# Expert gate/up of a mixture-of-experts layer: high and low token halves stacked in one stationary operand, two weight passes, the halves folded by a product

## The reference

```python
def expert_block(args):
    xb, e = args
    hb = jax.nn.silu(xb @ w_gate[e]) * (xb @ w_up[e])
    return hb @ w_down[e]
```

## Time and profile before

| | |
|---|---|
| runs shown, median of 3 | 2478.95 us (2477.13 to 2481.66) |
| the profiled execution: span from first to last instruction | 2474.9 us |
| the part before the first expert product | 1206 us |
| PE busy | 2220.9 us, 90% of the span |
| DVE busy | 1447.8 us, 58% |
| ACT busy | 1201.1 us, 49% |
| loads by SyncE's queue | 530.43 MB |

### The profile page before, as it was taken

One profiled execution on the slowest core, in us unless ns is written; L12 is line 12 of the kernel. 1 busy time (PEld: TensorE's weight loads), 2 busy tenths in 40 slices (PEclk: granted clock), 3 DMA queues, 4 the chain that ended last, 5 costly groups with the idle time before them and its releaser, 6 DMA issues.

```text
span 2474.9 us, 36169 instructions
## 1 busy us (share of the span) xinstructions
PE 2220.9 (90%) x13825; PEld 2005.5 (81%) x13825; DVE 1447.8 (58%) x1219; ACT 1201.1 (49%) x1121; POOL 233.6 (9%) x237
## 2 busy tenths in 40 slices
PE   2999999999999999995599999999999999999970
PEld 2989999999999999985477787787777778778750
DVE  8443232222222243337587887887887887887858
ACT  3333232222122232224377777777777777777743
POOL 4000440000000010003101000000000000000004
PEclk9999999999999999996799999999999999999985
DMA  6334233333323244336399999999999999999944
GB/s 225 85 98 112 69 94 88 91 89 89 92 86 93 85 151 131 106 100 241 113 344 359 357 352 355 361 351 349 359 354 354 358 358 347 368 360 350 371 176 170
DMA packets 338329, 556.23 MB, mean 225 GB/s; under 512 B 13592, under 2 KB 179552, under 8 KB 315360
## 3 DMA queue, kind: packets, MB, share of 16 engines
q1 hardware_dynamic: 330848, 530.43, 61.5%
q0 software_dynamic: 7440, 25.25, 3.4%
HBM read 542.78 MB, written 29.62 MB: 231 GB/s over the span
## 4 chain that ended last, share of the span: by engine, by line
PE 83%; DVE 8%; ACT 4%; issue 3%; DMA 1%; DVEq 0%; SPq 0%; ACTq 0%; POOLq 0%; POOL 0%
PE ps L1558 79%; ACT ehi L796 2%; PE ps L1787 2%; DVE hrow L1486 1%; DVE wlo L1109 1%; DVE eraw L1520 1%; PE ps L1750 1%; DMA rows<-in_x 1%; DVE rows L1130 1%; DVE nmr L1125 1%; PE ps L1795 1%; DVE xT_lo L1109 0%; ACT whi L796 0%; DVE eraw L1532 0%; DVE stats L1112 0%
## 5 line engine op out<-in xcount | busy, mean ns | idle before, releaser
L1109 DVE TENSOR_TENSOR elo<-eraw,ehi 128x2048 fp32r<-128x2048 f32 x380 | 856.6, 2289 | 146.6 <-ACT ehi L796 142.0
L796 ACT ACTIVATE ehi<-eraw 128x2048 fp32r<-128x2048 f32 x384 | 724.9, 1914 | 150.2 <-PE ps L1558 145.3
L1109 DVE TENSOR_TENSOR wlo<-raw,whi 128x1024 fp32r<-128x1024 f32 (+3 forms) x200 | 225.2, 1126 | 567.7 <-ACT whi L796 565.9
L796 ACT ACTIVATE whi<-raw 128x1024 fp32r<-128x1024 f32 (+3 forms) x200 | 191.6, 959 | 736.6 <-PE ps L1558 736.6
L1558 PE MATMUL ps<-act_hi,whi 128*128 128x264 f32 x2048 | 423.7, 287 | 18.7 <-DVE wlo L1109 13.4
L1558 PE MATMUL ps<-act_lo,whi 128*128 128x264 f32 x2048 | 422.0, 286 | 0.0
L1558 PE MATMUL ps<-act_hi,wlo 128*128 128x264 f32 x2048 | 421.8, 286 | 0.0
L1558 PE MATMUL ps<-ehi,xT_hi 128*128 128x512 f32 x1024 | 403.4, 394 | 4.7 <-DVE elo L1109 4.7
L1558 PE MATMUL ps<-ehi,xT_lo 128*128 128x512 f32 x1024 | 400.4, 391 | 0.0
L1558 PE MATMUL ps<-elo,xT_hi 128*128 128x512 f32 x1024 | 399.6, 390 | 0.0
L1558 PEld LDWEIGHTS ps<-act_hi,whi 128*128 128x128 f32 x2048 | 321.5, 189 | 21.2 <-DVE wlo L1109 12.1
(11 more groups left out here) (192 smaller groups left out, 2107.1 us busy)
## 6 DMA issues: line engine op xcount, KB each, us to landing
eraw<-in_w_gate SPq DMA_DIRECT2D x128, 1024.0 KB, 7.6
eraw<-in_w_up SPq DMA_DIRECT2D x128, 1024.0 KB, 7.8
eraw<-in_w_down SPq DMA_DIRECT2D x128, 1024.0 KB, 9.1
raw<-in_w_in SPq DMA_DIRECT2D x96, 512.0 KB, 3.8
raw<-in_w_out SPq DMA_DIRECT2D x32, 512.0 KB, 3.9
h_rows<-rows SPq DMA_DIRECT2D x8, 1024.0 KB, 7.3
raw<-in_w_branch_pool SPq DMA_DIRECT2D x16, 512.0 KB, 3.9
raw<-in_w_branch_fourier SPq DMA_DIRECT2D x16, 512.0 KB, 3.9
```

The costliest lines, as they stand in the source:

```text
L796: act.activation(dst, src, ACT.Copy, **kw).then_inc(done, 1)
L1109: dve.tensor_tensor(dst, src, hi, ALU.subtract).then_inc(done, 1)
```

## The change

- **Stacking.** xT becomes one buffer [128, 16, 2, 64]: for each of the 16 row pieces the 64 hi columns and the 64 lo columns of the tokens side by side, 128 stationary columns in all. Each weight half is then streamed once: ehi and elo, 2 matmuls where there were 3 (64 per round instead of 96). Bank rows 0 to 63 hold hi x w, rows 64 to 127 lo x w. lo x elo, which the kernel before leaves out, is now in the sum.
- **Fold.** ACT copies banks 0 and 1 to `gu` in SBUF. In the next round 8 small float32 products of gu with `fold` [128 x 64] (two identities on top of one another) add the halves and transpose in one step; the result, 4 x 64 columns of gate and as many of up, goes to bank 1. ACT makes `silT` = silu of the gate part, DVE `hraw` = silT * up part, ACT and DVE split hraw to hT_hi and hT_lo. silu and product so stand after the transposing step, on 256 columns instead of 512.
- **Loads.** gate_up gives partition p the rows 4p to 4p+3 of a chunk, one run of 8 KB. The tokens' columns must then be taken with a step of four: xT is made by 16 float32 products of `xrow[:, start:start+509:4]` with 64 columns of the identity, all before the down chunks, 8 pieces to a bank.
- **Order.** On ACT y_evac moves from behind ehi 3 to behind ehi 1; silu stands behind ehi 5, ht_split behind ehi 6; on DVE the gated product behind elo 5, the split behind elo 6. PE's first up product (chunk 4) waits for h_done (hraw written) instead of ht_lo.

The diff, cut to its core:

```diff
-    hrow = sb("hrow", [P, F], F32, 65536)
...
-    xT_hi = sb("xT_hi", [P, KC, P], F32R, 167936)
-    xT_lo = sb("xT_lo", [P, KC, P], F32R, 176128)
+    xT = sb("xT", [P, KC, 2, CAP], F32R, 167936)
+    gu = sb("gu", [P, 2, F], F32, 176128)
+    silT = sb("silT", [P, 4, CAP], F32, 180224)
+    hraw = sb("hraw", [P, 4, CAP], F32, 181248)
+    fold = sb("fold", [P, CAP], F32, 65536)
...
-    srow = sb("srow", [P, F], F32, 209088)
...
-            return w[0, bass.ds(e, 1), 512 * (i % 4):512 * (i % 4 + 1), :].rearrange("a (k p) n -> p (a k) n", p=P)
+            return w[0, bass.ds(e, 1), 512 * (i % 4):512 * (i % 4 + 1), :].rearrange("a (p k) n -> p (a k) n", p=P)
...
-                pool.wait_ge(xt_ready, 4 * b + 4)
+                pool.wait_ge(xt_ready, 2 * b + 2)
...
             def xt_evac(b, q):
-                act.wait_ge(xt_ready, 4 * b + q + 1)
-                copy(xT_hi[:, 4 * q:4 * q + 4, 0:CAP], used_cols(ps[:, 6 + q % 2, :]), xt_hi)
-            def ht_evac(b):
+                act.wait_ge(xt_ready, 2 * b + q + 1)
+                copy(xT[:, 8 * q:8 * q + 8, 0, :], xt_bank(q), xt_hi)
+            def gu_copy(b, a):
+                act.wait_ge(eused, number(b, 4 * a + 3) + (1 + ERING))
+                past(act, ht_ready, b)
+                copy(gu[:, a, :], ps[:, a, :], gu_done)
+            def silu(b):
                 act.wait_ge(ht_ready, b + 1)
-                copy(hT_hi[:, :, 0:CAP], used_cols(ps[:, 1, :]), ht_hi)
+                past(act, h_done, b)
+                act.activation(silT[:, :, :].rearrange("p c n -> p (c n)"), ps[:, 1, 0:4 * CAP], ACT.Silu).then_inc(silu_done, 1)
+            def ht_split(b):
+                act.wait_ge(h_done, b + 1)
+                copy(hT_hi[:, :, 0:CAP], hraw[:, :, :], ht_hi)
...
             def moe_round(b):
-                if not (isinstance(b, int) and b < 1):
-                    for i in range(4):
-                        ehi_chunk(b, i)
+                follows = not (isinstance(b, int) and b < 1)
+                if follows:
+                    ehi_chunk(b, 0)
+                    ehi_chunk(b, 1)
                 if not (isinstance(b, int) and b < 2):
                     y_evac(b - 2, number(b - 1, ECH - 1))
-                if not (isinstance(b, int) and b < 1):
-                    ht_evac(b - 1)
-                for i in range(4, 8):
-                    ehi_chunk(b, i)
-                act.wait_ge(eused, number(b, 3) + (1 + ERING))
-                past(act, h_done, b)
-                act.activation(srow[:, :], ps[:, 0, :], ACT.Silu).then_inc(silu_done, 1)
-                if not (isinstance(b, int) and b < 1):
+                if follows:
+                    ehi_chunk(b, 2)
+                    ehi_chunk(b, 3)
+                ehi_chunk(b, 4)
+                ehi_chunk(b, 5)
+                if follows:
+                    silu(b - 1)
+                ehi_chunk(b, 6)
+                if follows:
+                    ht_split(b - 1)
+                ehi_chunk(b, 7)
+                gu_copy(b, 0)
+                if follows:
                     for i in range(8, 12):
                         ehi_chunk(b, i)
-                for q in range(4):
+                gu_copy(b, 1)
+                for q in range(2):
                     xt_evac(b + 1, q)
...
             end = n_over + NE
             ehi_chunk(end, 0)
             ehi_chunk(end, 1)
-            ht_evac(end - 1)
+            silu(end - 1)
+            ht_split(end - 1)
             y_evac(end - 2, number(end, -1))
...
             def xt_evac(b, q):
-                dve.wait_ge(xt_hi, 4 * b + q + 1)
-                lo_of(xT_lo[:, 4 * q:4 * q + 4, 0:CAP], used_cols(ps[:, 6 + q % 2, :]),
-                      xT_hi[:, 4 * q:4 * q + 4, 0:CAP], xt_lo)
-            def ht_evac(b):
+                dve.wait_ge(xt_hi, 2 * b + q + 1)
+                lo_of(xT[:, 8 * q:8 * q + 8, 1, :], xt_bank(q), xT[:, 8 * q:8 * q + 8, 0, :], xt_lo)
+            def gated(b):
+                dve.wait_ge(silu_done, b + 1)
+                past(dve, ht_lo, b)
+                dve.tensor_tensor(hraw[:, :, :].rearrange("p c n -> p (c n)"), silT[:, :, :].rearrange("p c n -> p (c n)"),
+                                  ps[:, 1, 4 * CAP:8 * CAP], ALU.mult).then_inc(h_done, 1)
+            def ht_split(b):
                 dve.wait_ge(ht_hi, b + 1)
-                lo_of(hT_lo[:, :, 0:CAP], used_cols(ps[:, 1, :]), hT_hi[:, :, 0:CAP], ht_lo)
+                lo_of(hT_lo[:, :, 0:CAP], hraw[:, :, :], hT_hi[:, :, 0:CAP], ht_lo)
...
             def moe_round(b):
-                if not (isinstance(b, int) and b < 1):
+                follows = not (isinstance(b, int) and b < 1)
+                if follows:
                     for i in range(4):
                         elo_chunk(b, i)
-                if not (isinstance(b, int) and b < 1):
-                    ht_evac(b - 1)
-                for i in range(4, 8):
-                    elo_chunk(b, i)
-                if not (isinstance(b, int) and b < 1):
+                elo_chunk(b, 4)
+                elo_chunk(b, 5)
+                if follows:
+                    gated(b - 1)
+                elo_chunk(b, 6)
+                if follows:
+                    ht_split(b - 1)
+                elo_chunk(b, 7)
+                if follows:
                     for i in range(8, 12):
                         elo_chunk(b, i)
-                dve.wait_ge(silu_done, b + 1)
-                dve.wait_ge(eused, number(b, 7) + (1 + ERING))
-                past(dve, ht_lo, b)
-                dve.tensor_tensor(hrow[:, :], srow[:, :], ps[:, 1, :], ALU.mult).then_inc(h_done, 1)
-                for q in range(4):
+                for q in range(2):
                     xt_evac(b + 1, q)
-                if not (isinstance(b, int) and b < 1):
+                if follows:
                     gate_weights(b - 1)
-            for q in range(4):
+            dve.tensor_tensor(fold[:, :], ident[:, 0:CAP], ident[:, CAP:P], ALU.add).then_inc(fold_ready, 1)
+            for q in range(2):
                 xt_evac(0, q)
...
-            ht_evac(end - 1)
+            gated(end - 1)
+            ht_split(end - 1)
...
-            def xt(b, q):
-                if q == 0:
-                    pe.wait_ge(gathered, 16 * b + 16)
-                past(pe, xt_lo, 4 * b + q - 1 if q else 4 * b)
+            def xt(b):
+                pe.wait_ge(gathered, 16 * b + 16)
                 pe.wait_ge(pad_cols, 1)
-                for c in range(4):
-                    k = 4 * q + c
-                    last = pe.transpose(ps[:, 6 + q % 2, P * c:P * (c + 1)], xrow[:, P * k:P * (k + 1)], ident)
-                last.then_inc(xt_ready, 1)
+                for q in range(2):
+                    past(pe, xt_lo, 2 * b)
+                    for c in range(8):
+                        start = 512 * (2 * q + c // 4) + c % 4
+                        last = pe.matmul(xt_bank(q)[:, c, :], xrow[:, start:start + 509:4], ident[:, 0:CAP], start=True, stop=True)
+                    last.then_inc(xt_ready, 1)
             def ht(b):
-                pe.wait_ge(h_done, b + 1)
-                pe.wait_ge(pad_cols, 5)
-                for c in range(4):
-                    last = pe.transpose(ps[:, 1, P * c:P * (c + 1)], hrow[:, P * c:P * (c + 1)], ident)
+                pe.wait_ge(gu_done, 2 * b + 2)
+                pe.wait_ge(fold_ready, 1)
+                for a in range(2):
+                    for c in range(4):
+                        at_c = 4 * CAP * a + CAP * c
+                        last = pe.matmul(ps[:, 1, at_c:at_c + CAP], gu[:, a, P * c:P * (c + 1)], fold[:, :],
+                                         start=True, stop=True)
                 last.then_inc(ht_ready, 1)
             def down_product(b, i, k):
@@ -1809,34 +1825,30 @@
             def moe_round(b):
                 follows = not (isinstance(b, int) and b < 1)
                 for i in range(8):
-                    if i < 4:
-                        pe.wait_ge(xt_lo, 4 * b + i + 1)
+                    if i in (0, 2):
+                        pe.wait_ge(xt_lo, 2 * b + i // 2 + 1)
                     if i == 0:
-                        past(pe, silu_done, b)
+                        past(pe, gu_done, 2 * b)
                     if i == 2 and follows:
                         ht(b - 1)
                     if i == 4:
-                        past(pe, ht_lo, b)
+                        past(pe, h_done, b)
                     pe.wait_ge(elo_done, number(b, i) + 1)
                     for kk in range(4):
                         k = 4 * (i % 4) + kk
-                        last = product([ps[:, i // 4, :]], xT_hi[:, k, :], xT_lo[:, k, :],
-                                       [ehi[:, i % ERING, F * kk:F * (kk + 1)]],
-                                       [elo[:, i % ERING, F * kk:F * (kk + 1)]], k == 0, k == KC - 1)
+                        both = xT[:, k, :, :].rearrange("p a n -> p (a n)")
```

(28 more changed lines are left out.)

4 lines of the change are left out of this document (3 added, 1 removed).

## The result

| | before | change |
|---|---|---|
| median of 4 runs | 2478.04 us (2474.78 to 2481.66) | 2601.37 us (2598.68 to 2604.86) |
| span of the profiled execution | 2474.9 us | 2601.9 us |
| one expert round, mean of the 31 distances between gated products | 36.87 us | 40.63 us |
| one expert round, rounds 2 to 30, from first gate product to first gate product | 36.88 us | 40.97 us |

The ratio is 1.049 (95% interval 1.0463 to 1.0517). The change is slower by 5%, where I forecast 3% faster.

What follows compares the result with a forecast made beforehand. PE was taken to set the pace; rounds going from 36.87 to 33.30 us gave 107 less, start 5.6 less, end 2.3 more, clock 30 more: -80, 2394.6 us, given as 2398 after the runs' median, range 2360 to 2460.

Steps and rivals of the forecast that it cites:

- The loop: Expert round, last down product through yrow, ehi 2, elo 2 to 5, hraw, chunks 4 to 7, xT, down: 33.30 us.
- The loads are hidden: Expert-stage loads at 424 GB/s with gather and scatter: 31.5 us a round, under the 33.3 of the loop.
- the price of the xT products: Sixteen strided float32 products on PE per round, taken at 0.19 us each, 3.04 us in the loop.
- The prediction's own sign of being wrong: The prediction called itself wrong if, among other signs, PE's xT stretch took over 5 us.
- The break-even: Price of one strided xT product from which the change turns slower: 0.42 us.
- rival 5: The strided xT read costs four times, 0.76 us a product, 9.1 more per round: 2642 us; chance 0.08.
- rival 4: The strided xT read doubles the record, 3.0 us more per round: 2459 us; chance 0.13.
- clock term: PE's clock falls after the new stall in half of the rounds at 2 us, 1 us a round: 30 us more.
- If 367 stayed, 36.1: Expert-stage loads staying at 367 GB/s despite 8 KB runs, rounds of 36.1 us: 2453 us; chance 0.05.
- Start and end: Outside rounds 2 to 31: the start 5.6 us less, the end 2.3 us more.
- part of the rounds: PE's clock falls after the stall in only some rounds, the forecast case: 2398 us; chance 0.45.

Runs made afterwards that it cites:

- e1_contig: The change with contiguous xrow pieces and 2 KB runs again, stacking, fold and order kept: 2401.3 us, ratio 0.967.
- e3_transpose: The change with 14 of the 16 xT products made as one-pass transposes, 8 KB runs and step four kept: 2412.8 us, ratio 0.971.
- e6_fill: The change with 12 extra 512-column products on PE ahead of the wait for hraw: 2570.7 us, ratio 1.034.
- e7_both: e3_transpose with the order edit of e4_order added: 2323.3 us, ratio 0.937.
- e8_contig_order: e1_contig with the order edit of e4_order added: 2371.8 us, ratio 0.958.
- e4_order: The change with y_evac one chunk later and silu, product and split one chunk earlier on ACT and DVE: 2507.2 us, ratio 1.010.
- e10_double: e1_contig with every xT product made twice, the repeat writing the same values: 2528.5 us, ratio 1.020.
- e11_mix: e4_order with the sixteen strided xT products put one by one between the first down products: 2400.7 us, ratio 0.968.
- e2_step2: The change with 4 KB runs, so that xrow is read with a step of two elements: 2429.2 us, ratio 0.979.

## Why the prediction was wrong

**What held.** The gate and up products went from 96 to 64. The fold's eight products were put at 1.5 us and take 1.70. The loop is there as described: the trace shows yrow, ehi 2 right behind it, elo 2 to 5, hraw, then chunk 4. ACT and DVE around it, of one round:

```profile
1809.02 2.75 ACT L1044 ACTIVATE yrow<-ps,gcol 64x512 f32<-64x512 f32 x4 [1.51 <-PE ps L1571]
1811.66 7.32 ACT L783 ACTIVATE ehi<-eraw 128x2048 fp32r<-128x2048 f32 x4
```

```profile
1813.60 8.90 DVE L1114 TENSOR_TENSOR elo<-eraw,ehi 128x2048 fp32r<-128x2048 f32 x4 [3.77 <-ACT ehi L783]
1822.41 0.41 DVE L1471 TENSOR_TENSOR hraw<-silT,ps 128x256 f32<-128x256 f32 x1
```

DVE idle 3.77 us ahead of elo 2 (3.5 forecast), elo 2 to 5 in 8.90 (8.98), PE's stall 2.70 (about 3.0). From the last down product to chunk 4 the loop was put at 2.72 + 8.98 + 0.40 = 12.10 us; the gate products with the stall and the fold, which fill that time on PE, take 10.38 + 1.70 = 12.08. The loads are hidden, as said.

**The step that failed** is the price of the xT products: "I take 0.19, since the rows near it are the same operation". They were the same operation on a contiguous operand; the price under the step is 0.453, 7.26 us for the term put at 3.04. The prediction's own sign of being wrong, an xT stretch over 5 us, came. The break-even, which rival 5 gave as 0.42 us a product, was thus crossed, and the size lay between rival 4 (0.38) and rival 5 (0.76). That 0.42 left out the prediction's own clock term; with 1 us a round for it the break-even is (36.87 - 34.30 + 0.11) / 16 + 0.19 = 0.36. The argument against rival 5, that the weight load is partly hidden, was true but proved little: of 329 ns some 100 are hidden (records start 227 ns apart), hardly more than of the contiguous load (192, starts 109 apart), and the rest is paid.

e1_contig and e3_transpose take this one step away in two different ways and give 2401 and 2413 us, where 2398 was forecast. Part of that agreement is luck. In e1_contig the rounds without a fall take 34.03 us, 0.73 over the 33.30 of the loop: xT products 0.45 (0.218 a product, not 0.19), down and up products 0.31 (0.231 apart, not 0.227). The falls cost it 0.46 us a round where 1.0 was put. The two misses nearly cancel.

**The clock** was sized wrongly too. I put one fall, in half the rounds, 1 us a round. The change has two in a round: the one after the stall in nearly all rounds (1.33 us in the up products, by e6_fill), and one in the xT stretch (1.8 us: the first nine down products start 0.57 and then 0.40 to 0.43 apart instead of 0.32 and then 0.23). The second was in no case of mine. Rival 4 took a doubled record and falls after the stall, 2459 us, and came nearest in kind. With the measured terms in place the loop closes: 33.30 + 4.22 (xT) + 0.31 (down and up products as above) + 1.33 + 1.82 (the two falls) = 40.98, measured 40.97 in rounds 2 to 30.

**Loads.** "If 367 stayed, 36.1" was too high an end: e1_contig runs 34.17 with 2 KB runs, and when queued all the time these move more than in the row of 367 read from before.

```profile
1700.00:2200.00 500.00, 462.05 (x2330) 386.45 (x2329) 414.19 (x247) 395.92 (x317) 59.73 (x59) 0.98 1.02 379
```

The Trainium skill (DMA: Bandwidth & Descriptors, section Where 436 GB/s comes from) has HBM bind near 358 GB/s a core. For this kernel, which runs on one core alone, the traces speak against it: 407 GB/s over 700 us in e7_both, 379 over 500 us in e1_contig.

**Start and end** were put at 5.6 less and 2.3 more beyond the rounds 2 to 31. The change has 2.3 more ahead of round 2 and 2.1 more behind round 31 (beyond 30 x 4.09), so the end was right and the start was off: three xT stretches at the strided pace lie ahead of round 2. With contiguous pieces (e1_contig, whose round 2 begins at 1271.18 us) the start is 4.8 less and the end 1.3 more, near what was put.

**How I came to it.** The Trainium skill's rule on lines (SBUF — State Buffer, section Door 1: The DMA port swizzle) was before me and pointed at a dearer record, though it gives no price; I gave the doubled record 0.13 because no row showed it, and took the price from rows that could not show it either. Where a change makes one operand strided for the first time, the rows are silent on just that, and a warning that speaks of it deserved the larger part. And the sum's margin on this term, 0.23 us a product (0.17 with the clock term), was smaller than the distance between its two ends, 0.57.

## What to carry to other kernels

A layout that makes transfers cheaper hands the bill to whoever reads it: find that instruction, and price it with the step it will have. Float32 products from a stationary operand with a step of 16 bytes cost double here (0.227 us a record for 0.109), with a step of 8 almost nothing more (0.115), and a one-pass transpose hardly notices 16 (0.11 to 0.12 for 0.10). When steps that used to lie beside each other are put in series (fold, silu, product, split), look at what is queued ahead of them on each engine: one chunk's shift of y_evac, with silu and product one chunk earlier, was worth 3.4 us a round. Undo the parts of a losing change one at a time: e7_both is 155 us faster than the kernel before and 278 faster than the change; e8_contig_order, which mends the same two faults without the cheaper transposes, 109 and 230.

## What the runs showed of the hardware

- A busy PE can lose its clock: 7.26 us of strided float32 products went to 1.2 GHz in each round of the change, e4_order and e6_fill, with no stall ahead of it in the last two. As long a stretch of contiguous ones (e10_double) kept 2.4 GHz (1.00 over 7.20 us), and so did the strided ones mixed one to one with 512-column products (e11_mix, no fall in any mixed stretch). Why the slower pace loses it is open.
- The same stall of 2.7 us is followed by a fall in 30 of 31 rounds of the change, 27 of e3_transpose, 15 of e2_step2, 13 of e10_double and 6 of e1_contig. These are counts of one execution each; over the four of e2_step2 the mean granted clock goes from 0.951 to 0.941 and the time from 2420 to 2435 us, so they vary. What decides it is open; the forecast of "part of the rounds" fits e1_contig, e2_step2 and e10_double, not e3_transpose.
- The strided records keep their pace when the clock falls; the clock is not what limits them. The xT products of the change alone, in windows ahead of the fall and behind it (columns as above, PE's):

```profile
1832.00:1835.00 3.00, 3.00 (x15) 1.00 1.02 426
1836.00:1839.00 3.00, 3.00 (x14) 0.50 1.02 429
```

- Loads of 8 KB runs held 402 GB/s from 1240 to 2230 us of e7_both, nearly the whole expert stage. At 2 KB the same queue reached 384 (e8_contig_order, 1700 to 2200 us), where the kernel before, bound by PE, had shown 357 on average.
